# A three-block forward pass on one core: the mixer's scan tables moved into an earlier stage, its scan in 4-token blocks, its norm behind the projection, its output projection in halves

## What is computed

```python
def second_block(x, ...):
    h = x
    u = rmsnorm(h, norm_mix) @ w_in                       # 1024 -> 1024
    u_pool, u_ssm = u[..., :512], u[..., 512:]
    y_pool = pool_mixer(u_pool, w_pool, pool_scale)       # 4 groups of 128: mean over 2, 4, 8, 16 tokens
    y_ssm = ssm_mixer(u_ssm, ...)                         # 32 groups of 16 channels, 64 complex states each
    h = h + concat([y_pool, y_ssm]) @ w_out
    h = h + swiglu(rmsnorm(h, norm_ffn), w_gate, w_up, w_down)
    return rmsnorm(h, norm_final)

def ssm_mixer(u, ...):
    # s[t] = a * s[t-1] + B u[t]   (complex diagonal a);   y = Re(C s) + d * u
    y = gelu(y)
    return y * sigmoid(y @ w_glu + b_glu)
```

## Time and profile before

| | |
|---|---|
| median of 3 runs | 2555.01 us (2554.77 to 2555.15) |
| profiled execution | 2553.49 us, its span 2551.7 us |
| PE busy | 2377.5 us, 93% of the span |
| DVE, ACT, POOL busy | 38%, 38%, 46% |
| mean granted PE clock | 0.963 |
| memory read | 211 MB, 84 GB/s |

### The profile page before, as it was taken

How to read it: one execution, slowest core, us unless ns; L and a number is a source line. 1 busy time by engine, 2 the same in 40 slices (tenths; PEclk the granted TensorE clock), 3 DMA queues, 4 the chain that set the end, 5 groups by cost and what they waited for, 6 DMA issues and landing times. The chain is left out here.

```text
span 2551.7 us, 32695 instructions
## 1 busy us (share of the span) xinstructions
PE 2377.5 (93%) x11520; PEld 1943.8 (76%) x11520; DVE 978.8 (38%) x1448; ACT 981.1 (38%) x1326; POOL 1173.0 (46%) x705
## 2 busy tenths in 40 slices
PE   7999999999999997999999999999993749999998
PEld 5877888878888875888888878888872527788886
DVE  6355352343344015355352343344018973211101
ACT  4343343244555224344343244555223204444421
POOL 5677324544444441333324544444446675344452
PEclk9999999999999997999999999999995869999999
DMA  5211213222222321212213222222320202222321
GB/s 178 78 63 68 80 65 99 99 75 98 91 94 95 108 91 65 81 66 80 80 58 104 94 81 93 97 92 93 105 91 25 67 0 75 82 91 98 99 100 58
DMA packets 59974, 214.19 MB, mean 84 GB/s; under 512 B 7168, under 2 KB 7424, under 8 KB 59904
## 3 DMA queue, kind: packets, MB, share of 16 engines
q1 hardware_dynamic: 55872, 203.45, 23.9%
q10 hardware_dynamic: 4032, 9.81, 1.1%
HBM read 211.13 MB, written 2.10 MB: 84 GB/s over the span
## 5 line engine op out<-in xcount | busy, mean ns | idle before, releaser
L372 POOL TENSOR_TENSOR w_lo<-stage,w_hi 128x1024 fp32r<-128x1024 f32 x380 | 929.2, 2454 | 1251.4 <-ACT w_hi L1135 1239.3
L720 PE MATMUL psum<-xh,w_hi 128*128 128x512 f32 x1952 | 773.7, 396 | 43.3 <-DVE na_q_lo L1536 14.3
L720 PE MATMUL psum<-xl,w_hi 128*128 128x512 f32 x1952 | 766.9, 393 | 0.0
L720 PE MATMUL psum<-xh,w_lo 128*128 128x512 f32 x1952 | 766.6, 393 | 0.0
L1135 ACT ACTIVATE w_hi<-stage 128x1024 fp32r<-128x1024 f32 x377 | 396.7, 1053 | 339.1 <-PE psum L720 338.3
L720 PEld LDWEIGHTS psum<-xh,w_hi 128*128 128x128 f32 x1952 | 371.0, 190 | 131.2 <-DVE na_q_lo L1536 15.1
L720 PEld LDWEIGHTS psum<-xh,w_lo 128*128 128x128 f32 x1952 | 370.8, 190 | 78.5
L720 PEld LDWEIGHTS psum<-xl,w_hi 128*128 128x128 f32 x1952 | 371.5, 190 | 75.2
L720 PE MATMUL psum<-g_hi,w_hi 128*128 128x512 f32 x528 | 205.4, 389 | 0.0
L720 PE MATMUL psum<-g_lo,w_hi 128*128 128x512 f32 x528 | 205.4, 389 | 0.0
L720 PE MATMUL psum<-g_hi,w_lo 128*128 128x512 f32 x528 | 205.4, 389 | 0.0
(11 more groups left out here) (341 smaller groups left out, 3214.7 us busy)
## 6 DMA issues: line engine op xcount, KB each, us to landing
stage<-in_w SPq DMA_DIRECT2D x380, 512.0 KB, 3.3
bias<-in_bias ACTq DMA_DIRECT2D x8, 384.0 KB, 3.0
z<-in_x SPq DMA_DIRECT2D x4, 512.0 KB, 9.1
out_x<-out_t SPq DMA_DIRECT2D x4, 512.0 KB, 2.7
masks<-in_masks ACTq DMA_DIRECT2D x2, 576.0 KB, 6.1
rope<-in_rope ACTq DMA_DIRECT2D x2, 512.0 KB, 3.9
p_raw<-in_p ACTq DMA_DIRECT2D x2, 512.0 KB, 3.2
delta<-in_delta ACTq DMA_DIRECT2D x2, 448.0 KB, 4.6
```

Source lines behind the costliest of these rows:

```text
L372: pool.tensor_tensor(w_lo[s][:, :, :], stage[s][:, :, :], w_hi[s][:, :, :].bitcast(F32), ALU.subtract).then_inc(lo_done, 1)
L720: mm = pe.matmul(dst, lhs[i], rhs[j], start=start and n == 0, stop=stop and n == 2)
```

## The change

- **Tables in layer 1's down stage.** The powers of C (`c_first`, `c_power`) and the angle tables (`phase_level`, now cosines and sines both on DVE) are made between DVE's additions of the second layer's down stage. Their tiles lie in xh, which is free then. c_st is loaded at the start of that stage, b_st four roundings before its end. The convolution's matrices (`conv_kernel`) are made in two halves, one ahead of the sum of squares of the last layer norm, one ahead of the RMS norm's spread.
- **Blocks of 4 tokens.** BT = 4, NB = 128. A state tile has 128 x 512 elements, the scans 128 blocks. POOL makes three powers of B (`b_powers`), ACT spreads four.
- **All turns on DVE.** `state_im_part` is gone from POOL.
- **Norm behind the projection.** The last layer norm writes, for the mixer, the high and low parts of z times the norm's weight (xm_hi, xm_lo). The input projection starts on them. The scale of the RMS norm is made meanwhile, copied to rms_sb, and applied by DVE to the four scan results as it reads them, and by POOL to the four pool groups (one more product in `pooling`).
- **Output projection in halves.** The four weight blocks for the pool tiles and the four for the scan tiles of each output are separate passes: pool half of outputs 0 to 3 (ahead of the GLU), pool half of 4 to 7 (behind the GLU), then the scan half of all 8. Each half result is added to z. SP loads the units accordingly (`load_halves`).
- PE's order in the mixer is new, with the block inputs, convolutions and state products between the later projection units; state products and block inputs change their row or column group at every matmul. The layer loop on PE, ACT and DVE is written out.

The core of the diff:

```diff
-BT = 2
+BT = 4
...
-            with pe.Fori(0, DEPTH) as L:
+            for L in range(DEPTH):
...
 # POOL
+            for u in range(4):
+                mixer_low(u)
+            b_powers()
+            for u in range(4, 8):
+                mixer_low(u)
             pooling(0)
+            mixer_low(8)
             pooling(1)
-            state_im_part(1)
+            mixer_low(9)
             pooling(2)
+            mixer_low(10)
             pooling(3)
-            state_im_part(2)
-            state_im_part(3)
...
 # POOL, pooling(g)
+                tt(u, u, rms_sb[:, :], ALU.mult).then_inc(*pool_next())
...
 # PE, down_layer
                 mean(L * 2 + 1, after_result(L, DOWN_R0 + KT - 1))
+                if L == DEPTH - 1:
+                    pe.wait_ge(c_ready, 2 * BT + 2)
+                    pe.wait_ge(b_in, 16)
+                    conv_kernel(0)
+                    conv_kernel(1)
                 variance(L * 2 + 1, sq)
...
 # PE, mixer
+                first_units(MIX, MIN_U0, MIN_R0, n0 * KT, parts=xm_parts)
+                in_unit(2, Y_BANK)
+                variance(n0, sq_1)
+                conv_kernel(2)
+                conv_kernel(3)
+                spread(n0, rstd_1)
+                in_unit(3, O_BANK)
                 pe.wait_ge(wb_apart, 2 * BT)
+                pe.wait_ge(kernel_ready, 4)
                 block_inputs(0)
+                in_unit(4, take_bank(MIX, MIN_R0 + 4))
+                convolve(0)
                 block_inputs(1)
+                in_unit(5, take_bank(MIX, MIN_R0 + 5))
                 block_inputs(2)
+                in_unit(6, take_bank(MIX, MIN_R0 + 6))
                 from_state(0)
                 block_inputs(3)
+                in_unit(7, take_bank(MIX, MIN_R0 + 7))
+                convolve(1)
                 from_state(1)
+                pool_product(0)
+                pool_product(1)
                 convolve(2)
                 convolve(3)
+                pool_product(2)
+                pool_product(3)
                 from_state(2)
                 from_state(3)
+                half_units(MP_U0, MP_R0, 2, *pool_mix)
+                half_units(GLU_U0, GLU_R0, 2, *ssm_y)
+                half_units(MP2_U0, MP2_R0, 2, *pool_mix)
+                half_units(MS_U0, MS_R0, 4, *ssm_mix)
...
 # ACT, norm, where to_mixer is the last layer norm
+                if to_mixer:
+                    act.dma_start(w_b[:, BT - 1, :, :, :], a["w_b"]).then_inc(wb_in, 16)
+                    act.dma_start(w_pool[:], a["w_pool"]).then_inc(wp_in, 16)
+                    round_ahead(MIX, MIN_U0)
                 act.wait_ge(sq_used, n * KT + KT)
                 act.activation(rstd[:, 0:P], S_BANK[1][:, 0:P], ACT.Sqrt, bias=ln_eps[:, :]).then_inc(lstd, 1)
...
 # ACT, down stage
                     round_ahead(L, DOWN0 + k)
+                    if L == DEPTH - 1 and k == DOWN_U - 4:
+                        act.wait_ge(phase_c, LEVELS + 1)
+                        act.wait_ge(phase_s, LEVELS + 1)
+                        act.dma_start(b_st[:], a["b_st"]).then_inc(b_in, 16)
...
 # DVE, residual_down
+                    if L == DEPTH - 1 and m == 0:
+                        c_first()
+                    if L == DEPTH - 1 and m in (1, 2):
+                        c_power(2 * m - 2)
+                        c_power(2 * m - 1)
+                    if L == DEPTH - 1 and m == 3:
+                        phase_first()
+                        for l in range(LEVELS - 2):
+                            phase_level(l)
+                    if L == DEPTH - 1 and m in (4, 5):
+                        phase_level(LEVELS - 6 + m)
...
 # DVE, state_tiles: four products, two sums, scans, four products, two sums
+                tt(zr, vr, c, ALU.mult).then_inc(turned, 1)
+                tt(t0, vi, s, ALU.mult).then_inc(turned, 1)
+                tt(zi, vi, c, ALU.mult).then_inc(turned, 1)
+                tt(t1, vr, s, ALU.mult).then_inc(v_read, 1)
...
+                tt(t1, zr, s, ALU.mult).then_inc(state_part, 1)
+                tt(zr, zr, c, ALU.mult).then_inc(state_part, 1)
                 dve.wait_ge(scanned, 8 * q + 8)
+                tt(t0, zi, s, ALU.mult).then_inc(state_part, 1)
+                tt(zi, zi, c, ALU.mult).then_inc(state_part, 1)
...
 # DVE, mixer
+                dve.tensor_copy(rms_sb[:, :], S_BANK[0][:, :]).then_inc(rms_copied, 1)
+                dve.wait_ge(rms_copied, 1)
+                for m in range(SP_T):
+                    src = (*U_BANK, Y_BANK, O_BANK)[m]
+                    unit_result(MIX, MIN_U0 + m)
+                    dve.tensor_tensor(u_all[:, SP_T + m, :], src[:, :], rms_sb[:, :], ALU.mult).then_inc(bank_free[m % 2], 1)
```

More of the change, by code:

```diff
@@ L500, in coefficients @@
                 tt(s_mag, mg, mg, ALU.mult).then_inc(*step())
+                for _ in range(BT.bit_length() - 2):
+                    pool.wait_ge(*settled())
+                    tt(s_mag, s_mag, s_mag, ALU.mult).then_inc(*step())
                 tt(den, re, re, ALU.mult).then_inc(*step())
@@ L986, in down, with conv_kernel @@
                             mm.then_inc(mid_done, 1)
+            def conv_kernel(q):
+                for c in range(2):
+                    for m in range(4):
+                        r0 = m * 2 * SCH
+                        mm = pe.matmul(T_BANK[0][r0:r0 + 2 * SCH, q * 2 * SCH * BT:(q + 1) * 2 * SCH * BT], b_st[:, c, 4 * q + m, :],
+                                       c_pow[:, 4 * q + m, c, 0:BT, :].rearrange("p k n -> p (k n)"), start=c == 0, stop=c == 1)
+                mm.then_inc(kernel_done, 1)
             def down_layer(L):
@@ L1034, in from_state, with pool_product @@
                     mm.then_inc(y_done, 1)
[L1036 to L1040 removed]
+                def pool_product(g):
+                    dst = take_bank(MIX, WP_R0 + g)
+                    if g == 0:
+                        pe.wait_ge(wp_in, 16)
+                    pe.wait_ge(pooled, 2 * g + 2)
+                    pe.matmul(dst[:, :], w_pool[:, g, :], u_all[:, g, :], start=True, stop=True).then_inc(pool_done, 1)
@@ new lines, in half_units @@
+                def half_units(u0, r0, count, ready, parts):
+                    for m in range(2 * count):
+                        u = u0 + m // 2
+                        if m % 2 == 0:
+                            take_unit(MIX, u)
+                        dst = take_bank(MIX, r0 + m)
+                        for k in range(SP_T):
+                            pe.wait_ge(*ready(k))
+                            mm = passes(dst[:, :], wt(u, 4 * (m % 2) + k), parts(k), k == 0, k == SP_T - 1)
+                        mm.then_inc(unit_used if m % 2 else mid_done, 1)
@@ L1048, in mixer @@
-                for m in range(ST):
-                    q, r0 = m // 4, m % 4 * 2 * SCH
-                    for c in range(2):
-                        mm = pe.matmul(O_BANK[r0:r0 + 2 * SCH, q * 2 * SCH * BT:(q + 1) * 2 * SCH * BT], b_st[:, c, m, :],
-                                       c_pow[:, m, c, 0:BT, :].rearrange("p k n -> p (k n)"), start=c == 0, stop=c == 1)
-                mm.then_inc(kernel_done, 1)
-                pe.wait_ge(kernel_ready, 4)
-                convolve(0)
+                in_unit(5, take_bank(MIX, MIN_R0 + 5))
@@ L1360, in mixer @@
-                for g in range(SP_T):
-                    act.wait_ge(y_pool, g + 1)
-                    act.activation(mix_hi[:, g, :], u_all[:, g, :], ACT.Copy).then_inc(mix_hi_s, 1)
+                ahead(3)
+                ahead(4)
+                for m in range(SP_T, KT):
+                    raw_out(m)
+                    ahead(m + 1)
+                pool_out(0)
+                pool_out(1)
+                gelu_high(0)
+                gelu_high(1)
+                pool_out(2)
+                pool_out(3)
@@ L1431, in _ @@
             act.activation(decay_a[:, :], decay_a[:, :], ACT.Ln, bias=1.0).then_inc(decay_step, 1)
-            with act.Fori(0, DEPTH) as L:
+            for L in range(DEPTH):
                 act.wait_ge(x_lo, (L * 2 + 1) * KT)
@@ L1929, in _ @@
             dve.wait_ge(mpar_in, 16)
-            with dve.Fori(0, DEPTH) as L:
+            for L in range(DEPTH):
                 dve.wait_ge(tables_in, L * 48 + 48)
```

562 lines of the change are left out of this document (294 added, 268 removed).

## The result

The changed kernel takes **2464.77 us** (median of 4 runs, 2459.35 to 2465.57), the kernel before 2555.08 us beside it: ratio 0.9643, 95% interval 0.9631 to 0.9655. The forecast was 2468.5 with a range of 2450 to 2484: 3.7 us too high. That difference is what has to be explained.

What follows compares the result with a forecast made beforehand. PE bounds most of the kernel; the change targets 207 us before the GLU where PE is busy 110. Saving 86.4 us from the profiled 2553.5 gives 2467.1, plus 1.5 for the median: 2468.5, range 2450 to 2484.

Steps and rivals of the forecast that it cites:

- block inputs: Mixer, matmuls for state tile 0: 2.2 us as before, from the same number of columns; bounds 1.1 and 4.4.
- Layers unrolled instead of looped: 0: Layer loop written out: priced at 0 us, since the page's rows don't show that the loop costs anything.
- Rival (c): Unrolled layer 1: fetching PE's code afresh starves PE, slower than before; 10% is 90 us, 12% gives 2576; chance 0.02.
- Part 1: Tables in layer 1's down stage: hidden between DVE's additions at price 0, or a few us if cover is gone.
- Part 2: Mixer start, norm on the projection's output: first matmul at 1923.7 instead of 1959.5, tile 0's inputs done at 1957.7.
- Part 3: State tiles in blocks of 4, all on DVE: 18 us a tile beside POOL; half projection starts at 2029.
- the pool groups: POOL's pooling in the mixer: four groups of 5.6, 6.9, 8.2 and 9.5 us; 37.6 us alone with three low parts.
- rival (a): State tiles: DVE and POOL disturb each other less, half projection 9 us earlier at 2013 to 2022; 2452 to 2461; chance 0.26.
- PE waits last for DVE's states instead of POOL: Sign against the forecast, before the half projection: it expected PE's wait for POOL's u_all, near 2012 to 2020.
- Part 4: Output projection in halves: the same 240 passes at 0.2266 us, 54.4 us where the old order took 56.5.
- (d): Layer 1's down stage: tables don't hide; a missed rounding costs 5.4 us, two 11; chance 0.23 together with (b).
- (b): Mixer: total lock, short matmuls at upper bounds, or both; half projection at 2038 to 2046, 2477 to 2486; 0.23 with (d).

## Why the forecast was near, point by point

The difference of 7.75 us of the profiled executions has these parts, each from the windows and timelines above:

| part | forecast | measured | less than forecast |
|---|---|---|---|
| up to A | 1906.6 | 1901.03 | 5.6 |
| A to the half projection | 122.4 | 117.8 | 4.6 |
| the halves | 54.6 | 56.6 | -2.0 |
| rest | 381.6 | 382.0 | -0.4 |

**Up to A.** The step that failed is "Layers unrolled instead of looped: 0; the page's rows don't show that the loop costs anything". Rival (c) looked at it only as a danger. The page doesn't show it, but the timeline of the kernel before did: PE's wait of 13.21 us at the boundary, and 3.65 us on ACT ahead of its first load. It is worth 3 us. The other 2.6 are the scatter of the part ahead of A: over the ten profiles of the changed kernel and its variants A has its median at 1903.6, 3.0 below the forecast, and the one profile of the kernel before that gave the 1906.6 is a single draw too.

From A to the half projection, by its steps (us behind A):

| step | forecast | measured |
|---|---|---|
| first projection matmul | 17.1 | 16.3 |
| units 0 and 1 done | 32.9 | 31.0 |
| fourth unit starts | 43.4 | 40.9 |
| block inputs of tile 0 done | 51.1 | 50.4 |
| POOL's pooling ends | 113.9 | 108.8 |
| DVE's last state tile ends | 115.4 | 113.4 |
| half projection starts | 122.4 | 117.8 |

**Part 1** held. The down stage is busy to the end, its results still come 14.96 us apart, and the tables cost nothing that shows. The first half of the kernel matrices takes 1.08 us (1.1), which is luck in the way it was priced: these 16 matmuls cost 0.07 us each, and the block inputs, from whose columns the 1.1 was taken, 0.12.

**Part 2.** The first matmul came 0.8 us sooner, since ACT's two loads were hidden beside the squares: its root starts at A + 8.9 where it did at A + 8.4 before, 0.5 us later for the 1.3 forecast. The low parts at 1.25 us, 1.83 us apart, were forecast as 1.85. The **block inputs** are the mis-sized term of this part: 3.89 us instead of 2.2, because I priced them by columns, and twice as many matmuls of half the columns cost 1.8 times as much. It was inside the bounds of 1.1 and 4.4.

**Part 3.** Tile 0 takes 9.8 us (10.3 alone, and 13.3 as forecast beside POOL), the other three 21.2, 13.4 and 16.1, 50.7 together for 51. That these sums agree hides terms that don't follow from their rows. The 5.4 us for eight scans aren't the 1.45 of the earlier trace rows times 2.64, which is 3.8; the runs gave 4.83 to 6.18. And the pool groups, by the prices named for them, come to 5.1, 6.4, 7.6 and 8.8 us, 2.3 less than the 30.2 that were put in; gaps may be meant, but it names none. The rule that I took from the earlier trace rows, that the two engines alternate by whole instructions, is wrong in detail: instructions of DVE that follow each other without a gap can keep POOL out for their whole length (4.63 us in tile 0) and elsewhere let it in (1976.52), and the scans are slowed too (5.67, 6.18 and 4.83 us for eight, 2.62 alone). The Trainium skill (SBUF — State Buffer, "SBUF: two separate sides") speaks of exclusion for the whole instruction; for the two-input instructions the rows agree, the 2.87 beside a low part of 2.84, but the scans overlap in part: within the 5.67 us POOL gets through some 5 us of work, counted at what its instructions take alone, beside 2.62 of scans. POOL ends 5 us sooner than forecast, half of the way to rival (a). What the prediction named as a sign against itself, "PE waits last for DVE's states instead of POOL", came: DVE ends last, near its forecast, and the steps behind were mis-sized. I put 8.5 us between POOL's end and the projection (4.4 lie behind DVE's), with pool product 3 at 1.7 and the state products at 3.4 and 2.5 us; a state product takes 1.94 at full clock, and only one lies behind DVE. No row gave the 1.7 us for a state product at full clock, and it lies below the prediction's own bound of 1.8. The run with the old orders gives the bound of 5.9 that I had kept.

**Part 4.** The same 240 passes, and no wait in them. The 2.2 us above the 54.4 of the passes alone (the forecast's end at 2083.6 leaves them 54.6) are in the main nine passes 0.43 us apart instead of 0.227; the run with fillers removed 1.5 of them. I had allowed for the halved clock in the state products and not in the halves.

**Rivals.** The half projection, at A + 117.8, lies between (a) (2013 to 2022, A + 106 to 115) and the forecast (122.4); that the profiled time falls within (a)'s 2452 to 2461 comes from the part ahead of A. (c) and (d) did not show, of (b) only the dearer block inputs. That the forecast is good to 3.7 us is also luck in the signs: block inputs (1.7 us too low for the tile on the path) and the clock (2.2) stand against ACT's loop (3), the first operands and units (2.5), and the state products with what lies behind them (4).

## What to carry to other kernels

Look at the wait of the bounding engine where an outer loop turns, and at what the engines that load tables do there: a jump can stand on the path though no row on the page names it. Price matmuls with few columns from a row of the same shape and order, and not by columns: twice the number at half the columns made the block inputs 1.8 times as long, and the order alone made a state product three times as long. Let the column group change at each one. When two engines exclude each other, work taken from one helps only as long as the third, PE, has slack; count all three queues up to the same point, and look at the granted clock behind PE's last waits: here two of them, 4 us together, were paid again with 1.5 us.

## What the runs showed of the hardware that was not expected

A jump back of ACT's loop: 2.3 to 2.6 us. Gapless two-input instructions of DVE (0.60 us each) kept POOL's waiting one out for all their length in tile 0, 4.63 us for 1.3 of work, and in other places let it in behind the first or second. State products (32 matmuls of 127 columns into 32 rows each): 1.94 us with the group changed at each one, 5.91 with the groups in a row. Waits of PE as short as 1.56 and 2.40 us, with little between them, were followed by 3.6 us at a granted clock of 0.53; with f32 matmuls in those waits it stayed at 1.00.

Open: what in ACT's jump takes the time, why the version with all three loops written out gained less than ACT's alone, why the first 60 us scatter by 4 us, when POOL gets in between DVE's instructions, why the layer norm's spread finds the higher clock in two profiles of ten, and how much of the 0.4 us for the moved mean is DVE's and how much PE's, since both end together there.
